# Gate projections in pieces of one token block, another order at the start of the chunk inversion, and two masks multiplied in another place

## The reference

```python
h = rms_norm(x, norm_w); proj = h @ w_in
(dn_q, dn_k, dn_v, dn_z, dn_beta, dn_decay, sw_q, sw_k, sw_v, sw_z) = split(proj)
dn = gated_deltanet_bidir(silu(conv(dn_q, dn_k, dn_v)), dn_beta, dn_decay)   # both directions
dn = rms_norm(dn) * silu(dn_z)
sw = windowed_gqa_with_sinks(sw_q, sw_k, sw_v) * silu(sw_z)                  # window of 128
x = x + concat(dn, sw) @ w_out
# inside the delta rule, for each chunk, head and direction:
decay = exp(where(incl, g[:, None] - g[None, :], -inf))
m = where(strict, (k * beta) @ k.T * decay, 0)
t_inv = inverse(eye + m);  a_intra = where(incl, q @ k.T * decay, 0)
```

## Time and profile before

| | us |
|---|---|
| median of 3 runs | 1033.44 (1033.11 to 1039.5) |
| the profiled execution's own time | 1038.53 |
| its span, first to last instruction | 1036.4 |
| TensorE busy | 974.4 (94%) |
| VectorE busy | 492.6 (48%) |
| ScalarE busy | 474.3 (46%) |
| GpSimd busy | 438.6 (42%) |

### The profile page before, as it was taken

One profiled execution on the slowest core, in us unless ns is written; L12 is line 12 of the kernel. 1 busy time (PEld: TensorE's weight loads), 2 busy tenths in 40 slices (PEclk: granted clock), 3 DMA queues, 4 the chain that ended last, 5 costly groups with the idle time before them and its releaser, 6 DMA issues.

```text
span 1036.4 us, 12883 instructions
## 1 busy us (share of the span) xinstructions
PE 974.4 (94%) x5218; PEld 822.3 (79%) x5218; DVE 492.6 (48%) x828; ACT 474.3 (46%) x830; POOL 438.6 (42%) x246
## 2 busy tenths in 40 slices
PE   7999798689999999999998979999999999999997
PEld 5987576679999997787776758888888888888876
DVE  4057775486675454414246432533333333564444
ACT  6564566546545253434476541543333433342233
POOL 3538333460002554243577642263443444454440
PEclk9999999879999999999999999999999999999999
DMA  9513110000002026133312221233233232333212
GB/s 345 165 62 101 61 41 1 1 1 1 1 1 82 1 80 218 61 102 104 100 61 62 71 77 64 69 115 115 82 103 100 82 118 85 100 104 100 86 38 81
DMA packets 25306, 84.07 MB, mean 81 GB/s; under 512 B 3008, under 2 KB 3264, under 8 KB 25120
## 3 DMA queue, kind: packets, MB, share of 16 engines
q1 hardware_dynamic: 24240, 81.88, 24.2%
q10 hardware_dynamic: 1008, 1.38, 0.4%
HBM read 79.06 MB, written 2.10 MB: 78 GB/s over the span
## 4 chain that ended last, share of the span: by engine, by line
PE 79%; DVE 9%; ACT 6%; POOL 3%; issue 2%; DMA 0%; POOLq 0%; DVEq 0%; ACTq 0%
PE bank L1925 76%; PE bank L1933 4%; DVE qk L1476 2%; ACT wh L1137 1%; POOL wl L1027 1%; ACT L1137 1%; DVE vc L1476 1%; ACT qk L1137 1%; DVE xf L1470 1%; ACT sl L1137 1%; POOL mp L1068 0%; DMA pparams<-in_pp 0%; DVE mp L1470 0%; DVE mp L1641 0%; DVE kl L1470 0%
## 5 line engine op out<-in xcount | busy, mean ns | idle before, releaser
L1027 POOL TENSOR_TENSOR wl<-raw,wh 128x1024 fp32r<-128x1024 f32 (+1 forms) x130 | 311.2, 2398 | 379.7 <-ACT wh L1137 379.7
L1925 PE MATMUL bank<-xh,wh 128*128 128x512 f32 (+1 forms) x536 | 207.1, 386 | 3.1 <-POOL wl L1027 1.9
L1925 PE MATMUL bank<-xh,wl 128*128 128x512 f32 (+1 forms) x536 | 205.3, 383 | 0.0
L1925 PE MATMUL bank<-xl,wh 128*128 128x512 f32 (+1 forms) x536 | 205.2, 383 | 0.0
L1137 ACT ACTIVATE wh<-raw 128x1024 fp32r<-128x1024 f32 (+2 forms) x132 | 135.8, 1036 | 133.0 <-PE bank L1925 125.4
L1925 PE MATMUL bank<-wh,xh 128*128 128x512 f32 (+1 forms) x352 | 143.2, 407 | 13.4 <-DVE xl L1476 7.2
L1925 PE MATMUL bank<-wl,xh 128*128 128x512 f32 (+1 forms) x352 | 137.8, 392 | 0.0
L1925 PE MATMUL bank<-wh,xl 128*128 128x512 f32 (+1 forms) x352 | 137.6, 391 | 0.0
L1925 PEld LDWEIGHTS bank<-xh,wh 128*128 128x128 f32 x536 | 100.7, 188 | 24.3 <-issue 3.6
L1925 PEld LDWEIGHTS bank<-xh,wl 128*128 128x128 f32 x536 | 100.7, 188 | 20.1
L1925 PEld LDWEIGHTS bank<-xl,wh 128*128 128x128 f32 x536 | 100.8, 188 | 19.0
(11 more groups left out here) (250 smaller groups left out, 1550.7 us busy)
## 6 DMA issues: line engine op xcount, KB each, us to landing
raw<-in_wflat SPq DMA_DIRECT2D x126, 512.0 KB, 3.5
xt<-in_xt SPq DMA_DIRECT2D x8, 256.0 KB, 4.3
h<-in_x SPq DMA_DIRECT2D x4, 512.0 KB, 8.5
h<-in_x SPq DMA_DIRECT2D x1, 2048.0 KB, 8.3
gain<-in_pr SPq DMA_DIRECT2D x3, 512.0 KB, 3.5
consts<-in_cf SPq DMA_DIRECT2D x1, 1472.0 KB, 11.6
raw<-in_wflat SPq DMA_DIRECT2D x4, 272.0 KB, 12.3
kh<-kh SPq DMA_DIRECT2D x8, 128.0 KB, 2.3
```

The costliest lines, as they stand in the source:

```text
L1027: e.tensor_tensor(WL[u % NS][:, 0:n], RAW[u % NS][:, 0:n], WH[u % NS][:, 0:n].bitcast(F32), ALU.subtract).then_inc(w_lo.up(u), 1)
L1925: return e.matmul(o, l, r_, start=start, stop=stop, skip_group_check=part)
```

## The change

1. **Gates in pieces.** A generator `tok_pieces` replaces `tok_part` and the loop for `U_Z`. It puts the 16 pieces of a gate (unit by token block, six matmuls each) into the list one by one. In the fourth unit the `Silu` of a token block (`tok_end`, cut out of ACT's `tok`) stands right behind its piece, no longer behind all four. Behind the pieces of `U_SZ` stand one step of `g3` (after every fourth piece) and one of `g1` (from the fourth piece on); behind each piece of `U_Z` one of `g1`.
2. **Banks.** `g1` has three banks (5, 6, 7) where it had four; bank 4 belongs to the inversion.
3. **Decays.** Chunk 0's two decay steps stand behind pieces 0 and 3 of `U_Z` (before: behind its second and third unit), chunk 3's behind pieces 9 and 11 (before: behind the whole gate).
4. **Weights of the last gate** are prepared one unit further ahead.
5. **Start of inversion and attention.** Before, the decays of three chunks and the products k k and q k of all four came in one piece, and only then the first steps of the attention. Now the first scores come at once, the decays of chunks 1 and 2 and the second scores behind them, and then one step of the attention behind each `inv_kq` and each `inv_m`.
6. **Masks.** For chunks 0 and 3 POOL multiplies the mask `mb` with minus beta itself (four more multiplications of 128x512), and DVE does one multiplication of 128x512 in each direction where it did four of 128x128.

```diff
--- before.py
+++ after.py
@@ -583,44 +583,50 @@
     G.over((0, 1, 2, 3))
     g1 = in_turn(qk_norm(), to_tokens("v"), rope_turn(), to_tokens("k"))
 
-    def tok_part(u0, n, by, *sides):
+    def tok_pieces(u0, name):
         ids, i = G.ids, G.i
         G.over((0, 1, 2, 3))
         for tb in range(4):
-            G.take(("tok", u0, tb), by(tb))
+            G.take(("tok", u0, tb), (proj, (name, tb)))
         G.ids, G.i = ids, i
-        for k in range(4):
-            w_ahead(u0 + k + 2)
-            do("tok", u0, k, "n0", SLOT0, n)
-            for g, m in sides:
-                step(g, m)
-
-    G.over((4, 5, 6, 7))
-    tok_part(U_SZ, 512, lambda tb: (proj, ("sz", tb)), (g3, 1), (g1, 3))
+        for n in range(16):
+            k, tb = n // 4, n % 4
+            if tb == 0:
+                w_ahead(u0 + k + (2 if u0 == U_SZ else 3))
+            do("tok_b", u0, k, "n0", SLOT0, 512, tb)
+            if k == 3:
+                do("tok_end", u0, tb)
+            yield n
+
+    G.over((5, 6, 7))
+    BI.over((4,))
+    for n in tok_pieces(U_SZ, "sz"):
+        if n % 4 == 3:
+            step(g3)
+        if n > 2:
+            step(g1)
     gi = [invert(cb) for cb in (0, 3, 1, 2)]
-    BI.over((4,))
-    ids, i = G.ids, G.i
-    G.over((0, 1, 2, 3))
-    for tb in range(4):
-        G.take(("tok", U_Z, tb), (proj, ("z", tb)))
-    G.ids, G.i = ids, i
-    for k in range(4):
-        w_ahead(U_Z + k + 2)
-        do("tok", U_Z, k, "n0", SLOT0, 512)
-        step(g1, 4)
-        if k in (1, 2):
+    for n in tok_pieces(U_Z, "z"):
+        step(g1)
+        if n in (0, 3):
             step(gi[0])
+        if n in (9, 11):
+            step(gi[1])
     while step(g1):
         pass
-    step(gi[1], 2)
-    BI.over((0, 1, 2, 3, 4))
     gs = swa()
     for b in (5, 6, 7):
         BANK[("swa", b)] = (b, emptied[b])
-    for g in gi[2:]:
-        step(g, 2)
+    BI.over((0, 1, 2, 3, 4))
+    step(gs)
+    step(gi[2], 2)
+    step(gi[3], 2)
+    step(gs)
     for g in gi:
         step(g)
+        step(gs)
+        step(g)
+        step(gs)
     live = True
     while live:
         live = False
@@ -1053,7 +1059,12 @@
             W = WORK[cb]
             ee, mb = W["EE"][d][:], W["MB"][d][:]
             on.wait_ge(*inv_a.at(("ee", cb, d)))
-            e.tensor_tensor(h3(mb), h3(ee), bc4((cf("SL"), cf("SU"))[d]), ALU.mult).then_inc(inv_g.up(("mb", cb, d)), 1)
+            if cb in (1, 2):
+                e.tensor_tensor(h3(mb), h3(ee), bc4((cf("SL"), cf("SU"))[d]), ALU.mult).then_inc(inv_g.up(("mb", cb, d)), 1)
+                return
+            e.tensor_tensor(h3(mb), h3(ee), bc4((cf("SL"), cf("SU"))[d]), ALU.mult).then_inc(inv_g.up(("mb0", cb, d)), 1)
+            on.wait_ge(*inv_g.at(("mb0", cb, d)))
+            e.tensor_tensor(h3(mb), h3(mb), b4r(NBETA[:, d, cb, :]), ALU.mult).then_inc(inv_g.up(("mb", cb, d)), 1)
 
         def inv_turn_mask(cb):
             for d in range(2):
@@ -1259,26 +1270,29 @@
             if i < 3 or u0 in (U_OUT, U_OUT2):
                 return
             for tb in range(4):
-                b, _ = BANK[("tok", u0, tb)]
-                on.wait_ge(*dense.at((u0 + 3, tb)))
-                p = psum[b]
-                r = dict(scale=RS[0][:, tb:tb + 1])
-                if u0 == U_KV:
-                    on.wait_ge(*norm_v.at(("r", 0, tb)))
-                    act(BD[:, tb, :], p[:, 0:16], ACT.Copy, proj.up(("bd", tb)), **r)
-                    act(SWR[:, tb, 0:128], p[:, 16:144], ACT.Copy, proj.up(("k", tb)), **r)
-                    act(SV[:, tb, :], p[:, 144:272], ACT.Copy, proj.up(("v", tb)), **r)
-                else:
-                    if u0 == U_V2:
-                        p4 = p[:, :].rearrange("p (h g d) -> p h g d", g=2, d=64)
-                        v4 = VV[:, tb].rearrange("p (h g) n -> p h g n", g=2)
-                        act(v4[:, :, 0, 0:64], p4[:, :, 0], ACT.Copy, proj.up(("v2e", tb)))
-                        act(v4[:, :, 1, 64:128], p4[:, :, 1], ACT.Copy, proj.up(("v2h", tb)))
-                        continue
-                    name, dst, f = {U_Q: ("q", SWR[:, tb, 128:640], ACT.Copy), U_SZ: ("sz", MIX[:, tb, 512:1024], ACT.Silu),
-                                    U_Z: ("z", MIX[:, tb, 0:512], ACT.Silu)}[u0]
-                    on.wait_ge(*norm_v.at(("r", 0, tb)))
-                    act(dst, p[:, :], f, proj.up((name, tb)), **r)
+                tok_end(u0, tb)
+
+        def tok_end(u0, tb):
+            b, _ = BANK[("tok", u0, tb)]
+            on.wait_ge(*dense.at((u0 + 3, tb)))
+            p = psum[b]
+            r = dict(scale=RS[0][:, tb:tb + 1])
+            if u0 == U_KV:
+                on.wait_ge(*norm_v.at(("r", 0, tb)))
+                act(BD[:, tb, :], p[:, 0:16], ACT.Copy, proj.up(("bd", tb)), **r)
+                act(SWR[:, tb, 0:128], p[:, 16:144], ACT.Copy, proj.up(("k", tb)), **r)
+                act(SV[:, tb, :], p[:, 144:272], ACT.Copy, proj.up(("v", tb)), **r)
+                return
+            if u0 == U_V2:
+                p4 = p[:, :].rearrange("p (h g d) -> p h g d", g=2, d=64)
+                v4 = VV[:, tb].rearrange("p (h g) n -> p h g n", g=2)
+                act(v4[:, :, 0, 0:64], p4[:, :, 0], ACT.Copy, proj.up(("v2e", tb)))
+                act(v4[:, :, 1, 64:128], p4[:, :, 1], ACT.Copy, proj.up(("v2h", tb)))
+                return
+            name, dst, f = {U_Q: ("q", SWR[:, tb, 128:640], ACT.Copy), U_SZ: ("sz", MIX[:, tb, 512:1024], ACT.Silu),
+                            U_Z: ("z", MIX[:, tb, 0:512], ACT.Silu)}[u0]
+            on.wait_ge(*norm_v.at(("r", 0, tb)))
+            act(dst, p[:, :], f, proj.up((name, tb)), **r)
 
         def inv_decay(cb, d):
             ee = WORK[cb]["EE"][d][:]
@@ -1455,7 +1469,7 @@
             e.dma_start(ov[:, tb, 0:512], OUT[:, tb, 0:512]).then_inc(s_out[0], 16)
 
         return dict(begin=begin, x_split=x_split, rms_row=rms_row, prep=prep, prep_half=prep_half, stat=stat, split=split, conv=conv, square=square, qsum=qsum, qexp=qexp, to_tok=to_tok,
-                    gate1=gate1, gate2=gate2, rope_root=rope_root, rope_t=rope_t, tok=tok, inv_decay=inv_decay, inv_m=inv_m, inv_turn=inv_turn,
+                    gate1=gate1, gate2=gate2, rope_root=rope_root, rope_t=rope_t, tok=tok, tok_end=tok_end, inv_decay=inv_decay, inv_m=inv_m, inv_turn=inv_turn,
                     inv_d=inv_d, swa_s=swa_s, swa_t=swa_t, swa_o=swa_o, scan_keys=scan_keys, scan_v=scan_vn, scan_o=scan_o,
                     dn_sq=dn_sq, forget=forget, cum_a=cum_a, gelu=gelu, qk2=qk2, fa_exp=fa_exp, fa_t=fa_t, fa_o=fa_o_, fa_split=fa_split,
                     gm_root=gm_root, up_post=up_post,
@@ -1637,6 +1651,9 @@
             on.wait_ge(*inv_p.at(("k", cb)))
             for d in range(2):
                 on.wait_ge(*inv_g.at(("mb", cb, d)))
+                if cb in (0, 3):
+                    tt(MP[cb][:, d, :], psum[b][:, :], W["MB"][d][:], ALU.mult, inv_v.up(("m0", cb, d)))
+                    continue
                 for h in range(4):
                     t = e.scalar_tensor_tensor(hs(MP[cb][:, d, :], h), hs(psum[b], h), NBETA[:, d, cb, h:h + 1], hs(W["MB"][d], h), ALU.mult, ALU.mult)
                 t.then_inc(inv_v.up(("m0", cb, d)), 1)
```

## The result

| | before | with the change |
|---|---|---|
| median of 20 runs each, us | 1034.67 (1033.11 to 1039.5) | 1037.18 (1035.2 to 1038.42) |
| ratio of the times | | 1.0019, 95% interval 1.0011 to 1.0028 |
| profiled execution, us | 1038.53 | 1037.33 |
| its span; mean granted clock | 1036.4; 0.982 | 1035.5; 0.979 |

The medians lie 2.5 us apart; the ratio over all runs, 1.0019, is 2.0 us (1.1 to 2.9). The forecast was 1029.6, in a range of 1023 to 1037; the time is just outside it. The difference to the forecast, 7.6 us, has three parts that the table separates: execution against execution the change gained 1.2 us where the sum said 3.8 (2.6 us), the profiled execution of before stands 3.9 us above its own median and that of the change 0.15 above its own (3.7), and the median of before is 1.2 higher over 20 runs than over three.

The account below looks back on a forecast made before the run. TensorE, busy 94% of the span, bounds the kernel, so only its idle or slow-clocked time can be gained. +1.2 us up to A and -5.0 from A to B give -3.8: median 1033.44 to 1029.6, range 1023 to 1037.

Parts of the forecast that it names:

- Part 1: First gate, 119.7 to 150 us: first sum waits for bank 5 instead of running in a hole; +0.7 us.
- Part 2, table loads: ScalarE, 144 to 164 us: eight loads instead of three around the Silu; 8 to 9 us of new TensorE holes.
- drain of some 1.38 us a switch: ScalarE table switches: the skill's surcharge, making 2.66 us a switch and the estimate about 1039; the forecast used 1.28.
- the last rotated transposes can start at about 176.0, when VectorE has done the second pair: Second gate on TensorE: from 176.0 the remaining work follows without a wait, giving A at 189.95 with no dip.
- A: Point where the second gate's last unit and decays of chunks 0 and 3 are done; before 190.2, forecast 191.4.
- Part 2, the dip: Second gate: holes between 152 and 167 us lower the clock, mostly within waits; 1.5 us carried.
- Part 3: Start of inversion and attention, A to B: 30.0 us including 3.4 of dips, before 35.0; -5.0 us.
- B: Point where the first product of the inversion's first level starts; before 225.23, forecast about 222 us.
- Part 4: Masks on VectorE and GpSimd: VectorE's saving and GpSimd's 5.0 us more leave the time unchanged; 0.
- that the clock stays up: Rival, 25%: new holes up to B bring no dips; to about 1024.7 us, with half of them 1027.
- That the wait only moves: Rival, 17%: at the attention's start nothing is gained; total +1.2, between 1031.5 and 1035.5 us.
- The slower case: Rival, 12%: last logarithm to `khh`, ScalarE bounds the second gate as switches cost more than their rows; 1033 to 1039.

Follow-up runs that it names:

- rope_early: The change with the last two rotary steps of the first gate behind pieces 9 and 10 instead of 11 and 15; 1029.54 us.
- prep_later: The change with every weight preparation under the second gate two pieces later; 1038.21 us.
- silu_pairs: The change with the first gate's four Silu two by two, behind pieces 13 and 15; 1030.58 us.
- silu_block: The change with the first gate's four Silu in one block behind its last piece, six table loads fewer; 1030.11 us.
- rope_block: The change with both the earlier rotary steps and the four Silu in one block; 1025.0 us.
- start_only: The kernel before with only the change's new start of inversion and attention; 1029.65 us.
- masks_only: The kernel before with only the change's new mask multiplications for chunks 0 and 3; 1033.92 us.
- base_again: The kernel before, unedited, profiled a second time in one execution; 1038.83 us.

## Why the prediction was wrong, step by step

- **Part 1, +0.7 us: right.** The wait is one of 5.21 us where there were 0.78 and 3.34, with the first sum behind it, and the gate ends at 149.93, or 150.3 with the 0.4 us by which the stretch began earlier (150.0).
- **Part 2, table loads: right.** Last `Silu` done at 163.14 (163.05), waits of 1.48, 2.37 and 2.35 us for 1.4, 2.7 and 3.6; the 0.9 for the first rotated transposes did not come, since the pieces ahead of them ran at half clock. The rival that ScalarE's loads cost more than their rows fell with it. So did the Trainium skill's drain of some 1.38 us a switch ("ScalarE: Activation LUTs", section What ACT_TABLE_LOAD costs): from 144 to 163 us of the change's trace eight loads follow each other, and each time the next instruction, a `Silu` or an exponential, starts 1.29 us after the load's start.
- **Part 2, "the last rotated transposes can start at about 176.0, when VectorE has done the second pair": this step failed.** They started at 180.63. The sentence named VectorE's second pair (of subtractions into `qhl`) and gave the way to it no timeline: that the change puts the last rotary step behind three more products that wait for exponentials was in the order of the queue, and was not carried through. The sum has no term for the step; its instructions come to 3.3 us without GpSimd beside them, and took 7.5. And by standing ahead of chunk 0's `ee` it stopped ScalarE for 4.67 us. The second pair was done at about 180.3. Behind it the forecast held: 14.1 us from the last rotated transposes to A, 13.95 in the sum. `rope_early` is the test of this step: with the rotary step out of the way they start at 174.70, released by VectorE's `qhl` as the sentence said, and A is at 188.83. Its stretch began 0.9 us earlier than that of before (124.05 for 124.98); with this added, 175.6 and 189.8 stand against 176.0 and the 189.95 that the sum gave without a dip. That its time of 1029.54 also meets the forecast is luck, since the reference was off (below).
- **Part 2, the dip: 1.5 us carried, 5.2 measured** (6.3 with what fell into the wait for `vt`, which ended at 163.68, forecast 163.6). The three holes of 1.5 to 2.4 us came within 10 us of each other, the fourth of 2.10 while the clock was still low. This is no second loss beside the late transposes: it lies ahead of 180.63. A at 191.4, measured 194.7, or 195.1 with the 0.4 us.
- **Part 3, B minus A 30.0: right to 0.1, in part by luck.** 225.35 - 194.7 = 30.6, with the 0.6 us of extra work taken off 30.0. The holes are others (0.60, 2.55, 0.24, 1.88 and 1.81, together 7.1, for 3.0 and 4.45), and low clock costs 4.1 us for 3.4. Five other profiled kernels have this order behind A and nearly the same holes, and took 28.5 (`rope_early`, `prep_later`), 30.1 (`silu_pairs`), 30.8 (`silu_block`) and 32.4 us (`rope_block`), according to how long the clock was low. `start_only` confirms by itself that the new start gains (4.7 us).
- **Part 4, 0: right** as far as `masks_only` can tell.
- **The reference.** The sum was made against an execution with a mean clock of 0.982; the common one has 0.985. The 3.0 us of dips that the sum let vanish with the holes of 2.09 and 2.87 were not there to be gained. The profile gave the sign: its time stood 5.1 us above the median of the three runs. The prediction carried this as a constant and did not ask where in the program it lay. Beside `masks_only`, 3.2 us of it lay between the stretch's start and A, 1.2 between A and B.

The rivals: that the clock stays up did not come (it got worse). Its argument "against", that holes of 2 to 3 us brought dips, held for the profiled execution and not for `masks_only`. That the wait only moves had its mechanism in the attention, and the loss lay ahead of A. The slower case, spread from 1033 to 1039, is nearest in time, but not in mechanism: its sign was a last `Silu` over 5 us later than 163.05, and that stood at 163.14.

## What to carry to other kernels

When work is put into smaller pieces, follow each side engine's queue past every wait that the new order adds, and ask what ready step now stands behind it; here a rotary step that had nothing to do with the exponentials cost about as much as six table loads (5.1 and 4.5 us, each with the other repaired). Repairs of a shared stretch must be tried together as well as alone: each alone looked like the whole answer. And where a profiled execution stands well off the median, find the windows that make the difference before subtracting from them.

## What the hardware showed that was not expected

- The same holes (2.09 and 2.87 us) in the same order of TensorE's work came with a granted clock between 0.57 and 0.63 in the next 3-us windows in two profiled executions (`before`, `base_again`) and at a clock of 1.00 in two others (`masks_only`, `start_only`). Likewise low clock behind A cost 1.5 us in `rope_early` and 5.7 in `rope_block`, at nearly the same holes. What decides it was not tried.
- Two float32 additions on VectorE, of 128x128 and 128x512, took 5.10 us (2.35 and 2.83) beside two subtractions of GpSimd (4.84 together) and 0.90 without; in the kernel before, a product of 128x640 took 2.99 us beside one and 0.82 without. GpSimd's row beside it there:

```profile
148.24 2.51 POOL L1027 TENSOR_TENSOR wl<-raw,wh 128x1024 fp32r<-128x1024 f32 x1 [0.27 <-ACT wh L1137]
```

The cost lies in who runs beside, not in the instruction.
